# A hybrid GLA / RWKV block pair on one core: first weight unit in three pieces, GLA matmuls by head pairs, four early f32 matmuls

## The reference, cut to what matters

```python
def rmsnorm(x, g):
    return x * rsqrt(mean(x * x, -1) + 1e-6) * g

# h = 16 meta tokens followed by x: 528 tokens
z = rmsnorm(h, norm_mix) @ w_in
a, q, k, v, r, lr, ga, gb = split(z)
log_a = log_sigmoid(lr @ w_gate_up + b_gate) / 16
# GLA: 4 heads of 64 key and 128 value columns, chunks of 64 tokens
b = cumsum(log_a)                                          # within a chunk
scores[t, s] = sum_k q[t,k] * k[s,k] * exp(-|b[t,k] - b[s,k]|)
o = scores @ v + (q * exp(b)) @ S                          # S: state of earlier chunks
S = exp(b_end) * S + (k * exp(b_end - b)).T @ v
o = rmsnorm(o, gla_norm) * silu(r)
m = sigmoid(ga) * y_a + sigmoid(gb) * (o @ w_gla_out)      # y_a: pooled branch of a
```

## Time and profile before

| | |
|---|---|
| time before, median of 3 runs | 1655.64 us (1653.81 to 1657.84) |
| the profiled execution, its own time | 1656.81 us |
| its span | 1654.8 us |
| mean granted TensorE clock | 0.982 of full speed |
| PE busy | 1591.1 us, 96% of the span |
| DVE, ACT, POOL busy | 820.8, 604.0, 394.9 us |
| DMA | 146.03 MB, mean 88 GB/s |

### The profile page before, as it was taken

The page is one execution under the profiler, slowest core; times in us unless marked ns, Lnnn a source line. Parts: engine busy times, 40 slices in busy tenths (PEclk is TensorE's granted clock), DMA queues, the critical chain, the costliest instruction groups (busy, mean ns, idle before and its releaser), DMA issues.

```text
span 1654.8 us, 26865 instructions
## 1 busy us (share of the span) xinstructions
PE 1591.1 (96%) x11510; PEld 1311.5 (79%) x11510; DVE 820.8 (50%) x1242; ACT 604.0 (36%) x967; POOL 394.9 (24%) x326
## 2 busy tenths in 40 slices
PE   5999999999999999999999988899999999999997
PEld 5899778887888888888877766779779888888876
DVE  2877541445433333335569987647537432333334
ACT  4344332334422313134355553435345332222222
POOL 2212011202210102024137443004013430330234
PEclk9999999999999999999999998999999999999998
DMA  5224321124222222222322100014212222222211
GB/s 207 103 84 166 109 76 40 67 86 153 89 102 88 92 100 96 88 96 95 129 95 78 52 4 3 29 59 146 77 51 78 77 102 102 94 84 102 102 60 68
DMA packets 29829, 146.03 MB, mean 88 GB/s; under 512 B 4096, under 2 KB 7440, under 8 KB 14608
## 3 DMA queue, kind: packets, MB, share of 16 engines
q1 hardware_dynamic: 29712, 144.33, 24.6%
HBM read 138.03 MB, written 6.29 MB: 87 GB/s over the span
## 4 chain that ended last, share of the span: by engine, by line
PE 78%; DVE 10%; issue 7%; POOL 2%; ACT 2%; DMA 1%; SPq 0%; POOLq 0%; DVEq 0%
PE ps L169 78%; DVE zf L181 3%; DVE wl L181 2%; POOL zf L181 2%; DVE ps L189 2%; DVE zf L189 1%; ACT zf L175 1%; DVE zr L189 1%; PE ps L172 1%; DVE zf L2316 1%; DMA raw<-in_wstream 1%; SPq L192 0%; ACT wh L178 0%; POOL tn L181 0%; ACT zf L178 0%
## 5 line engine op out<-in xcount | busy, mean ns | idle before, releaser
L169 PE MATMUL ps<-zr,wh 128*128 128x512 f32 (+3 forms) x4048 | 1175.4, 376 | 16.7 <-DVE wl L181 11.8
L169 PEld LDWEIGHTS ps<-zr,wh 128*128 128x128 f32 (+1 forms) x4048 | 730.0, 190 | 165.7 <-issue 16.8
L169 PE MATMUL ps<-zr,wl 128*128 128x512 f32 (+3 forms) x2024 | 753.7, 372 | 0.0
L181 POOL TENSOR_TENSOR zf<-zf 128x512 f32<-128x512 f32 (+1 forms) x237 | 286.0, 1213 | 775.5 <-ACT zf L175 518.9
L169 PEld LDWEIGHTS ps<-zr,wl 128*128 128x128 f32 (+1 forms) x2024 | 383.4, 189 | 72.1
L181 DVE TENSOR_TENSOR wl<-raw,wh 128x1024 fp32r<-128x1024 f32 (+1 forms) x243 | 307.8, 1306 | 195.6 <-ACT wh L178 195.4
L178 ACT ACTIVATE wh<-raw 128x1024 fp32r<-128x1024 f32 (+1 forms) x243 | 240.4, 1038 | 192.8 <-PE ps L169 191.4
L175 ACT ACTIVATE zf<-zf 128x512 f32<-128x512 f32 (+2 forms) x232 | 127.4, 561 | 371.5 <-DVE zf L181 258.8
L169 PE MATMUL ps<-zf 64*64 64x64 f32 (+6 forms) x3768 | 169.3, 244 | 21.2 <-issue 9.2
L181 DVE TENSOR_TENSOR zf<-ps,zf 128x512 f32<-128x512 f32 (+4 forms) x172 | 98.2, 578 | 175.4 <-PE ps L169 150.9
L169 PEld LDWEIGHTS ps<-zf 64*64 64x64 f32 (+3 forms) x3768 | 131.9, 147 | 61.7 <-issue 39.1
(11 more groups left out here) (82 smaller groups left out, 591.8 us busy)
## 6 DMA issues: line engine op xcount, KB each, us to landing
raw<-in_wstream SPq DMA_DIRECT2D x117, 1024.0 KB, 4.8
zf<-in_xT SPq DMA_DIRECT2D x16, 256.0 KB, 2.8
raw<-in_wstream SPq DMA_DIRECT2D x4, 768.0 KB, 4.3
kv_scratch<-zf SPq DMA_DIRECT2D x8, 256.0 KB, 2.2
x_scratch<-zf SPq DMA_DIRECT2D x8, 256.0 KB, 2.1
zf<-x_scratch SPq DMA_DIRECT2D x8, 256.0 KB, 4.4
out<-zf SPq DMA_DIRECT2D x16, 128.0 KB, 1.7
zf<-in_cu SPq DMA_DIRECT2D x1, 1256.0 KB, 10.9
```

The source lines that it names most:

```text
L169: return self.raw.matmul(out_, l, x, start=start, stop=stop)
L181: return self.raw.tensor_tensor(out_, a, b, o)
```

## The change

1. The first unit (tag `a`, the first 256 columns of `w_in`) gets another layout (kind `K`: k outermost) and is loaded, copied and subtracted in three pieces of 256, 768 and 1024 columns (`piece`; k = 0, k = 1 to 3, k = 4 to 7). The opening DMAs are reordered, meta tokens first, in a layout made on the host in which each partition has one run of 512 bytes; `cu`, `pmix` and `gup` move behind the next unit's load (`pro.2`).
2. Squares are woven between the `xs` steps on ACT; the meta statistic's square comes first on ACT, in a buffer of its own (`mg2`), and its reduction on DVE (`sum.im`) behind the split of unit 1. `cols` and `spread` steps of both statistics move.
3. `kw` issues, per k, four matmuls of wh x high, then four of wh x low, then four of wl x high, each group with a wait of its own.
4. `warm`: four f32 matmuls of 128 x 224 on the vectors' tile, into bank 7, before the first product; nothing reads them.
5. `gla.score(lv, tp)` alternates the two parities, and `gla.out(i)` makes two heads in one step, alternating them; each parity has its own rows and its own bank. The step list has two steps fewer in `gla.out`.

```diff
-    pair("a", "w_in", 0, 2)
+    t("a", "w_in", 0, 8, (0, 128), 128, "K")
+    t("a", "w_in", 0, 8, (256, 384))
...
     put("pro")
-    for k in range(8):
+    pl.loaded |= {0, 1}
+    pl.cut |= {0}
+    put("warm")
+    put("mg")
+    put("sq.im")
+    put("xs", 0)
+    put("ms")
+    for k in range(1, 8):
+        if k in (1, 2, 4):
+            put("piece", 0, k // 2)
         put("xs", k)
-        if k == 0:
-            pl.loaded |= {0, 1}
-            put("ms")
-            pl.split(0)
+        if k >= 5:
+            put("sq.in", k - 5)
+    put("sq.in", 3)
     n = pl.next_unit("a")
-    put("sq.im")
-    for k in range(8):
+    put("sum.im")
+    put("pro.2")
+    for k in range(4, 8):
         put("sq.in", k)
...
         put("kw", n, 0, k)
-        if k == 3:
+        if k == 6:
             pl.cols("in.rm")
-        if k == 6:
-            pl.spread("in.rm")
...
     a_tile(0, 0)
+    pl.cols("in.rs")
     a_tile(0, 1)
-    pl.cols("in.rs")
+    pl.spread("in.rm")
+    pl.spread("in.rs")
     pl.next_unit("a")
     a_tile(1, 0)
-    pl.spread("in.rs")
...
+            def warm():
+                e.wait_ge(("in.v",))
+                for i in range(4):
+                    e.mm(banks[7][:, 0:224], V[:, 0:128], V[:, 0:224])
...
-            def gla_score(lv, tp, par):
-                z, lo = 2 * tp + par, 64 * par
-                K = ("gla.sc", lv, z)
+            def gla_score(lv, tp):
...
                     for i in range(2):
-                        t = e.mm(ps(*K)[:, (2 * tl + i) * 128:(2 * tl + i + 1) * 128], kk[i][lo:lo + 64, cs],
-                                 qq[i][lo:lo + 64, cs])
-                t.then_inc(*e.up("mm", *K))
+                        for par in range(2):
+                            K, rows_ = ("gla.sc", lv, 2 * tp + par), slice(64 * par, 64 * par + 64)
+                            t = e.mm(ps(*K)[:, (2 * tl + i) * 128:(2 * tl + i + 1) * 128], kk[i][rows_, cs], qq[i][rows_, cs])
+                            if (tl, i) == (1, 1):
+                                t.then_inc(*e.up("mm", *K))
...
-            def gla_out(h):
-                i, hh = h // 2, h % 2
-                b = ps("gla.o", h)
-                e.wait_ge(freed("gla.o", h), ("gla.sc", 6, 3), ("gla.s", 7), ("gla.s", 0), ("gla.qh", 1))
+            def gla_out(i):
+
+                for hh in range(2):
+                    e.wait_ge(freed("gla.o", 2 * i + hh))
+                e.wait_ge(("gla.sc", 6, 3), ("gla.s", 7), ("gla.s", 0), ("gla.qh", 1))
                 for tt in range(4):
                     cs = slice(tt * 128, (tt + 1) * 128)
-                    e.mm(b[:, cs], F(29 + tt)[:, h * 128:(h + 1) * 128],
-                         SC[2 * (tt // 2) + hh][:, (2 * (tt % 2) + i) * 128:(2 * (tt % 2) + i + 1) * 128], stop=False)
+                    for hh in range(2):
+                        h = 2 * i + hh
+                        e.mm(ps("gla.o", h)[:, cs], F(29 + tt)[:, h * 128:(h + 1) * 128],
+                             SC[2 * (tt // 2) + hh][:, (2 * (tt % 2) + i) * 128:(2 * (tt % 2) + i + 1) * 128], stop=False)
...
+            def sum_im():
                 e.wait_ge(("in.msq",))
-                e.raw.tensor_reduce(msq[:, :], mg.rearrange("p k t -> p t k"), mybir.AxisListType.X,
+                e.raw.tensor_reduce(msq[:, :], mg2.rearrange("p k t -> p t k"), mybir.AxisListType.X,
                                     ADD).then_inc(*e.up("in.mq"))
```

More of the change, by code:

```diff
@@ L390, in bg_gla @@
                     pl.take("M", "gla.sc", lv, 2 * tp + par)
+                put("gla.score", lv, tp)
                 for par in range(2):
-                    put("gla.score", lv, tp, par)
                     pl.rel("M", "gla.sc", lv, 2 * tp + par)
@@ L416, in bg_gla @@
             yield
[L417 to L420, removed]
+        for i in range(2):
+            for hh in range(2):
+                pl.take("M", "gla.o", 2 * i + hh)
+            put("gla.out", i)
+            for hh in range(2):
+                pl.rel("M", "gla.o", 2 * i + hh)
             yield
@@ L1824, in tensor @@
             run(e, {
-                "mm": mm, "mw": mw, "kw": kw, "kt": kt, "ko": ko, "mh": mh, "koh": koh, "rows": rows, "cols": cols, "spread": spread, "gla.gate": gla_gate,
+                "mm": mm, "warm": warm, "mw": mw, "kw": kw, "kt": kt, "ko": ko, "mh": mh, "koh": koh, "rows": rows, "cols": cols, "spread": spread, "gla.gate": gla_gate,
                 "gla.score": gla_score, "gla.turn": gla_turn, "gla.turnm": gla_turnm, "gla.state0": gla_state0,
@@ L1862, in sq_im @@
             def sq_im():
-                e.wait_ge(("in.ms",))
-                e.act(mg, mh[:, :, :], ACT.Square).then_inc(*e.up("in.msq"))
+                e.wait_ge(("in.mh",))
+                e.act(mg2, mh[:, :, :], ACT.Square).then_inc(*e.up("in.msq"))
             def spread(s):
@@ L2183, in scalar @@
             run(e, {
-                "split": split, "xs": xs, "ms": ms, "sq.in": sq_in, "sq.im": sq_im, "spread": spread, "gla.gate": gla_gate,
+                "split": split, "piece": piece, "xs": xs, "ms": ms, "sq.in": sq_in, "sq.im": sq_im, "spread": spread, "gla.gate": gla_gate,
                 "gla.log": gla_log, "gla.exp": gla_exp, "gla.ends": gla_ends, "gla.turn": gla_turn,
@@ L2708, in vector @@
             run(e, {
-                "split": split, "xs": xs, "ms": ms, "sq.im": sq_im, "cols": cols, "ev.a": ev_a, "ev.k": ev_k, "ev.lr": ev_lr,
+                "split": split, "piece": piece, "xs": xs, "mg": mg_, "ms": ms, "sum.im": sum_im, "cols": cols, "ev.a": ev_a, "ev.k": ev_k, "ev.lr": ev_lr,
                 "ev.q": ev_q, "ev.v": ev_v, "cu": cu_, "pool": pool, "gla.gate": gla_gate, "gla.scan": gla_scan,
@@ L2866, in pro, with x, piece, pro_2 @@
             def pro():
-                e.dma(V[:, 0:NV], vecs).then_inc(*e.landed("v", "in.v"))
-                e.dma(F(0), xv[:, 0, :]).then_inc(*e.landed("x0", "in.xd", 0))
-                load(0)
-                e.dma(mh[:, :, :], metaT.rearrange("(k p) t -> p k t", p=P)).then_inc(*e.landed("mh", "in.mh"))
-                for k in range(1, 8):
-                    e.dma(F(k), xv[:, k, :]).then_inc(*e.landed(f"x{k}", "in.xd", k))
+                w0 = wstream[0:P * unit_size(UNITS[0])].rearrange("(p n) -> p n", p=P)
+                def x(k):
+                    e.dma(F(k), xv[:, k, :]).then_inc(*e.landed(f"x{k}", "in.xd", k))
+                def piece(c):
+                    a, b = cut_list(0)[c]
+                    e.dma(raw[0][:, a:b], w0[:, a:b]).then_inc(*e.landed(f"w0{c}", "w.in", 0, c))
+                e.dma(mh[:, :, :], metaT.rearrange("p (k t) -> p k t", t=16)).then_inc(*e.landed("mh", "in.mh"))
+                e.dma(V[:, 0:NV], vecs).then_inc(*e.landed("v", "in.v"))
+                x(0)
+                piece(0)
+                x(1)
+                piece(1)
+                x(2)
+                x(3)
+                piece(2)
+                for k in range(4, 8):
+                    x(k)
+                load(1)
                 e.dma(C[:, :], cf).then_inc(*e.landed("cf", "in.cf"))
-                load(1)
+            def pro_2():
                 e.dma(cu_raw, cu).then_inc(*e.landed("cu", "in.cu"))
```

74 lines of the change are left out of this document (53 added, 21 removed).

## The result

The change takes **1631.55 us** (median of four runs, 1630.83 to 1632.97) beside 1656.74 for the kernel before on the same chip (four runs): ratio 0.985, 95% interval 0.983 to 0.987. A second set gave 1630.92 (three runs) beside 1655.30. The profiled execution of the first set took 1632.97 us, with a span of 1630.9 against 1654.8. Two far slower runs stand in no median here, one of 2553.55 us in the second set and one of 3075.70 us of the kernel without the f32 matmuls; the others of these kernels lie within 6 us of each other.

The account below looks back on a forecast made before the run. PE carries 78% of the chain that ended last, though DVE sets the end in part of the score region. First stage 12.0, scores 3.3 + 3.3 and gla.out 6.2 sum to 24.8 off 1655.6: 1631 us, range 1623 to 1640.

Parts of the forecast that it names:

- first stage: Opening through the two `a` units: they end at 36.8 us against 48.8, -12.0 us (bounds -15 and -9).
- scores ahead of `mix`: Eight score steps at 112 to 163 us, largely paced by DVE: -3.3 us of 4.4 (bounds -0.6 and -4.4).
- scores behind `mix`: Six score steps behind 176 us, where ACT and DVE wait for PE: 0.55 us saved each, -3.3 us.
- gla.out: GLA output steps: the 64-row matmuls of two heads overlap, 15.9 us become 9.7, -6.2 us (bounds -2.7 and -8).
- A stretch of 2.8 may do that too: +1.0: First stage: PE's 2.8 us idle before k = 7 may drop the clock to half, costing 1.0 us.
- Wrong [...] if `a` ends after 40: First stage: the forecast counts as wrong if the `a` units, expected done at 36 to 37 us, end after 40.
- Half-filled work stays, so I book nothing: gla.out: the clock fell to 0.60 after the first step before the change; no gain from clock was booked.
- (a): First stage: `cols` of `in.rm` and POOL's chain stall PE, half clock to 30 us; -5 not -12, 1638; chance 0.15.
- (b): GLA: pairs with 128 weight columns each do not overlap; scores 0, gla.out -2.7, 1641 us; chance 0.12.
- (c): All gains come through: DVE freed, no idle before k = 7, no half clock after gla.out; 1623 us; chance 0.15.
- (d): Scores and gla.out: each change of row half drains the array, 0.2 us each; slower, 1667 us; chance 0.03.
- (e): First stage: the early pieces land with the bulk, so the change does not do what it says; 1643 us; chance 0.03.

Follow-up runs that it names:

- section 1: First stage of the change, every GLA step as in the kernel before, gla.out in four steps of 24: 1644.81 us, ratio 0.9939.
- the bad undo: The change with each score and gla.out step issuing one head's matmuls before the other's, same step list: 1654.92 us, ratio 0.9992.

## Why the prediction came out right

By its own steps, with the two traces and the runs:

| step | predicted | measured | by |
|---|---|---|---|
| first stage | 12.0 | 8.6 to 8.8 | both traces of the change; 8.8 alone |
| scores ahead of `mix` | 3.3 | 4.1 | only GLA, scores serial |
| scores behind `mix` | 3.3 | 3.2 to 3.3 | kernels with the same clock there |
| gla.out | 6.2 | 5.6 | 7.2 less the 1.6 that came without pairs |
| clock behind `mix` and gla.out | 0 | 1.6 + 1.6 | as above |
| sum, at the gates | 24.8 | 24.8 | |

- **First stage: mechanism right, size off.** Start, new wait, its place and its releaser came as written. Two terms failed. "The reduction ends near 20.5": it ended at 21.8, as the split began at 18.10, behind GpSimd's first addition at 15.01 and ScalarE's copy at 17.03; its length was priced rightly. And "A stretch of 2.8 may do that too: +1.0": the half clock cost 3.0. The rows held 6 us at half rate after the start, and the trace of the kernel before had a nearer price, behind its wait of 5.11 us that ends at 30.62: half clock until 35.0, TensorE busy for 4.4 us of it. One window of it:

```profile
32.00:36.00 4.00, 4.00 (x23) 4.00 (x23) 0.00 (x0) 1.74 (x2) 0.00 (x0) 0.63 0.20 68
```

- **Its own sign of being wrong.** "Wrong [...] if `a` ends after 40": it ended at 40.4 us, and at 40.2 in the second set. By that sign the first stage was forecast wrongly, although the total was right.
- **Scores.** The step of 1.09 us was 1.16; the half-and-half idea holds. Of the 4.4 on the DVE-bound side 4.1 came through, more than booked, since the contention with GpSimd eased as described, by 0.9 a split where 0.7 was booked. The wait before the po units did not grow to 4, because DVE gained as much as TensorE.
- **gla.out.** 4.84 predicted for two heads, 4.90 measured. The working has a flaw that did no harm: 1.8 us in the full-row matmuls and 2.6 in the others make 4.4, and the step takes 3.98, as the busy times of two forms that overlap don't add up. "Half-filled work stays, so I book nothing" was the unsafe sentence: no kernel with pairs lost the clock here, though neither did the one with four serial steps of section 1.
- **Rivals.** (a) 1638, little from the first stage: it has the mechanism that acted, but took 7 from the 12 where 3.4 went. (b) fell: the 64x64 form halved and the 64x128 form went from 23.9 to 16.3. The Trainium skill ("TensorE: Matmul & The Clock Gate", "LDWEIGHTS (loading the stationary operand)") prices a load by its columns; 16 of 128 columns would be 1.7 us by the prediction's estimate if they queued up. A paired step of 16 instructions takes 1.16, so they do not all queue here. (c) asked for more than came. (d), draining at each change of row half, fell by the same row. (e) fell by the first product at 6.28.
- **Luck.** The trace shows +3.2 of clock that nobody had booked against −3.4 of first stage. Without the cancelling the forecast was good to some 3 us, which the range covered. The +3.2 rests on one trace of the kernel before; whether its other executions had the same half-clock stretches is not on record.

## What to carry to other kernels

Matmuls of 64 rows that alternate between the two row halves overlap, also with 128 weight columns each (16 in 1.16 us in place of 1.71, the 64x64 form in half its time): look for them wherever heads are half as wide as the array. A wait removed from a chain shows the next one: before moving a step, list every engine that the stage waits for in turn (here DVE's reduction, then GpSimd's additions to 26.9 us), as TensorE only arrives earlier. And when undoing one part of a change, keep the kernel before's grouping of steps too, or the experiment tests something new.

## What the hardware showed beyond that

- The same wait does not always cost the same. All fourteen traces wait 3.05 to 3.16 us ahead of `mix`. In nine of them the clock falls to half within 1.5 us of the first product behind it (the kernel before among them, the first stage alone, either GLA part serial again, and all kernels with a sum or its reduction moved); in five it stays at 1.00 (the change twice, only GLA by pairs, without the f32 matmuls, and the bad undo). Where it falls late, the first two products still run at the full rate: with serial scores they took 1.12 us at 166.24, and from 167.5 to 170.7 the clock was 0.50 with TensorE busy throughout. The stretch costs 1.6 us, and which trace has it follows no edit near it.
- The wait for `msq` differs too. With the change's first stage and a wait of 3.56 us, the kernel with serial outputs had a clock of 0.50 from 22.9 to 26.1 us and 1.00 from 26.3 on, where the change ran at half until 28; its `a` stage was 9.4 us ahead.
- The clock also fell with TensorE 100% busy: 48 serial matmuls of gla.out in one piece took 9.5 to 11.4 us, twice in each of two kernels, against 7.96 for two steps of 24 at full clock. No idle stretch stood right before. What it is about these pieces (half-filled matmuls, their number in a row) was not varied by itself.
- GpSimd's seven additions took 11.90 us in the change and 9.77 in the kernel before. Two of them, beside DVE's two subtractions, took 2.15 and 2.07 us, alone 1.28; such a chain must be priced with what runs beside it.
